# Four gated branches over a Strassen-like input projection on one NeuronCore: merged sums in the loaded buffer, full fp32 memory products, whole-row norms on VectorE, and moved hooks

## What is computed

```python
proj = x @ w_in                       # 1024 -> 10*512 + 4*1024 columns
(q_sb, k_sb, v_sb, g_sb, u_pool, g_pool, u_lru, g_lru, q_xa, g_xa, merge) = _split_columns(proj)
y_sb = stick_breaking_attention(q_sb, k_sb, v_sb) * silu(g_sb)     # 4 heads of 128
y_pool = multiscale_pool(u_pool, w_pool, pool_scale) * silu(g_pool)
y_lru = rg_lru(u_lru, conv_w, conv_b, w_rg, b_rg, w_ig, b_ig, lru_L) * silu(g_lru)
y_xa = memory_cross_attention(q_xa, mem, w_mem_kv) * silu(g_xa)    # k, v = mem @ w_mem_kv
gates = sigmoid(merge.reshape(b, s, 4, 1024))
merged = gates[:, :, 0] * (y_sb @ w_branch[0])
for n in range(1, 4):
    merged = merged + gates[:, :, n] * (branches[n] @ w_branch[n])
out = layer_norm(2 ** 0.5 * x + merged @ w_out, ln_g, ln_b)
```

## Time and profile before

| | |
|---|---|
| median of 2 runs | 2663.57 us (2662.22 to 2664.92) |
| profiled execution, its own time | 2661.26 us |
| its span | 2659.5 us, mean granted PE clock 0.97 |
| PE busy | 2459.5 us, 92% |
| DVE busy | 1598.3 us, 60% |
| ACT busy | 1196.0 us, 45% |
| POOL busy | 1177.7 us, 44% |
| DMA | 257.10 MB, mean 97 GB/s |

### The profile page before, as it was taken

The page is one execution under the profiler, slowest core; times in us unless marked ns, Lnnn a source line. Parts: engine busy times, 40 slices in busy tenths (PEclk is TensorE's granted clock), DMA queues, the critical chain, the costliest instruction groups (busy, mean ns, idle before and its releaser), DMA issues.

```text
span 2659.5 us, 30199 instructions
## 1 busy us (share of the span) xinstructions
PE 2459.5 (92%) x10496; PEld 1955.0 (74%) x10496; DVE 1598.3 (60%) x2060; ACT 1196.0 (45%) x1832; POOL 1177.7 (44%) x764
## 2 busy tenths in 40 slices
PE   6999999999888989999899999999999888989898
PEld 5777778777667767777677777688777667767787
DVE  7677734843774365454787787734843774366354
ACT  5566632332662245222477677733342662245231
POOL 1566544743344333424365555544743344333332
PEclk9999999999999999999999999999999999999999
DMA  5443222123112311262332333222123112312243
GB/s 203 131 130 125 92 95 68 56 103 113 44 61 76 128 41 57 84 261 87 112 108 91 99 115 99 77 83 80 56 103 113 44 62 75 128 45 73 87 158 103
DMA packets 129255, 257.10 MB, mean 97 GB/s; under 512 B 12880, under 2 KB 74320, under 8 KB 128080
## 3 DMA queue, kind: packets, MB, share of 16 engines
q1 hardware_dynamic: 123056, 246.25, 27.5%
q10 hardware_dynamic: 6048, 8.92, 1.0%
HBM read 196.92 MB, written 58.20 MB: 96 GB/s over the span
## 4 chain that ended last, share of the span: by engine, by line
PE 58%; DVE 10%; issue 8%; POOL 4%; DMA 4%; ACT 4%; SPq 0%; ACTq 0%; POOLq 0%; DVEq 0%
PE J L648 11%; PE J L649 11%; PE J L650 11%; PE Z L816 6%; PE ACC L816 3%; PE OB L816 3%; DMA pk_m<-ST 3%; PE OB L786 3%; DVE WL L1529 1%; POOL SR L2034 1%; PE Z L648 1%; PE Z L649 1%; PE Z L650 1%; PE ACC L764 1%; DVE PR L1859 1%
## 5 line engine op out<-in xcount | busy, mean ns | idle before, releaser
L648 PE MATMUL J<-XBH,WHS 128*128 128x512 f32 x1152 | 479.4, 416 | 112.4 <-ACT ST L1031 64.0
L649 PE MATMUL J<-XBL,WHS 128*128 128x512 f32 x1152 | 468.3, 407 | 0.0
L650 PE MATMUL J<-XBH,WLS 128*128 128x512 f32 x1152 | 466.3, 405 | 0.0
L2041 POOL TENSOR_TENSOR WLS<-SR,WHS 128x1024 fp32r<-128x1024 f32 x121 | 319.7, 2642 | 145.0 <-ACT WHS L972 132.5
L648 PEld LDWEIGHTS J<-XBH,WHS 128*128 128x128 f32 x1152 | 228.3, 198 | 180.6 <-ACT ST L1031 72.4
L648 PE MATMUL J<-XBH,WH 128*128 128x512 f32 x864 | 343.4, 398 | 9.5 <-DVE XBL L1469 5.5
L649 PE MATMUL J<-XBL,WH 128*128 128x512 f32 x864 | 337.6, 391 | 0.0
L650 PE MATMUL J<-XBH,WL 128*128 128x512 f32 x864 | 337.0, 390 | 0.0
L1505 DVE TENSOR_TENSOR ST<-J,ST 128x512 f32<-128x512 f32 x160 | 109.5, 687 | 275.5 <-ACT ST L1031 156.8
L650 PEld LDWEIGHTS J<-XBH,WLS 128*128 128x128 f32 x1152 | 228.0, 198 | 50.9
L649 PEld LDWEIGHTS J<-XBL,WHS 128*128 128x128 f32 x1152 | 228.5, 198 | 48.7 <-issue 1.9
(11 more groups left out here) (363 smaller groups left out, 5231.6 us busy)
## 6 DMA issues: line engine op xcount, KB each, us to landing
RAW<-w SPq DMA_DIRECT2D x144, 512.0 KB, 3.7
MB<-pk_m SPq DMA_DIRECT2D x48, 512.0 KB, 6.0
pk_m<-ST SPq DMA_DIRECT2D x42, 512.0 KB, 5.1
KR<-pk_k SPq DMA_DIRECT2D x160, 128.0 KB, 2.2
BRAW<-w SPq DMA_DIRECT2D x64, 256.0 KB, 6.4
VR<-pk_v SPq DMA_DIRECT2D x160, 64.0 KB, 2.0
XRAW<-xt SPq DMA_DIRECT2D x8, 1024.0 KB, 13.1
OR<-w SPq DMA_DIRECT2D x16, 512.0 KB, 6.7
```

Source lines behind the costliest of these rows:

```text
L648: nc.tensor.matmul(to, wh, xh, start=first, stop=True, skip_group_check=True)
L649: nc.tensor.matmul(to, wh, xl, start=False, stop=True, skip_group_check=True)
L650: return nc.tensor.matmul(to, wl, xh, start=False, stop=True, skip_group_check=True)
L2041: G_.tensor_tensor(WLS[:, k, :], SR[:, k, :], WHS[:, k, :].bitcast(F32), ALU.subtract).then_inc(s_lo, 1)
```

## The change

What it does, part by part:

- **Merges.** For n > 0 `add` writes into `MB[f % 2]` in place, and for n = 0 `gated` writes there; stores go out from MB. ACT's first copy into a reused GT waits for the add that read the gate (`merged`, or `mu_done` for n = 0) and no longer for the store. Instead SP's `load_merged` for f >= 2 waits until the store of f-2 from the same MB has landed, and in `exchange` both stores stand ahead of both loads. `gated` of n = 0 waits for the store of f-2.
- **Pool weights** `WPR`, `WPH`, `WPL` and `LNG` get other addresses; WPR is loaded at hook 3 of the first pool pair and split at hook 10.
- **Memory keys and values** are full fp32 matmuls of `MW` and `MRAW` (32 of 256 columns and 16 of 512, in place of 96 and 48), with no splits. CRAW and PRM are loaded last of the first loads. The copy of the values to `VMA` goes from DVE to ACT.
- **Norms.** DVE scales the whole row of 1024; only the last row of all keeps ACT's `scale` and POOL's `finish`. The last two rows of the first half are finished at DVE hooks 2 and 5 of pair 37 (before: one ahead of pair 36, one at its hook 9).
- **First weights of the second half.** POOL makes all four sums, WL, WLS, WL2 and the second WLS between row products, and ACT's splits stand there too; pair 36 then needs none of these from DVE.
- **Hooks.** Mixing (PE) 6 to 8; `memory_turned` 8 to 10 on PE and DVE, `memory_values` 11 to 13, DVE's queries 10 to 11, silu 11 to 12; for n = 2 `split_y` 5 to 3 and `rest_y` 9 to 6.
- **LRU and M2.** The rest of the second weight sum goes from DVE to POOL there; that of the first stays on DVE.

```diff
             def load_merged(half, n, f):
-                wait_kept(sp, half, n - 1, f)
-                wait_if(sp, merged, add_count(half, n, max(f - 1, 0)))
+                if f < 2:
+                    wait_kept(sp, half, n - 1, f + 6)
+                elif n == NB - 1 and f - 2 >= KEPT:
+                    sp.wait_ge(merged, add_count(half, n, f - 1))
+                else:
+                    wait_kept(sp, half, n, f - 2)
                 sp.dma_start(MB[f % 2][:], pk_m[f]).then_inc(mb_in[f % 2], 16)
...
-                sp.dma_start(pk_m[f], GT[f % 4][:]).then_inc(m_kept[f % 4], 16)
+                sp.dma_start(pk_m[f], MB[f % 2][:]).then_inc(m_kept[f % 2], 16)
...
                 for j in (f, f + 1):
                     if n < NB - 1 or j < KEPT:
                         keep_merged(half, n, j)
-                    if n and j + 2 < FT:
-                        load_merged(half, n, j + 2)
+                for j in (f + 2, f + 3):
+                    if n and j < FT:
+                        load_merged(half, n, j)
...
+            def gates_read(half, n, f):
+                if n:
+                    act.wait_ge(merged, add_count(half, n, f) + 1)
+                else:
+                    act.wait_ge(mu_done, f_count(half, n, f) + 1)
...
                 elif kind == "merge" and i >= 2:
-                    wait_kept(act, half, n, 2 * i + p - 4)
+                    gates_read(half, n, 2 * i + p - 4)
...
-                    mm = V_.tensor_tensor(GT[f % 4][:, s], BR[f % 2][c][:], GT[f % 4][:, s], ALU.mult)
+                    to = GT[f % 4][:, s] if n else MB[f % 2][:, s]
+                    mm = V_.tensor_tensor(to, BR[f % 2][c][:], GT[f % 4][:, s], ALU.mult)
...
-                to = MERGED[:, f, :] if n == NB - 1 and f >= KEPT else GT[f % 4][:]
+                to = MERGED[:, f, :] if n == NB - 1 and f >= KEPT else MB[f % 2][:]
...
-                    mm = pass3(KBANK[h][:, 0:MEM], (KWH[h][:, k, :], KWL[h][:, k, :]), (MTH[:, k, :], MTL[:, k, :]),
-                               k == 0)
+                    mm = nc.tensor.matmul(KBANK[h][:, 0:MEM], MW[:, h, k, :], MRAW[:, k, :], start=k == 0,
+                                          stop=k == KD - 1)
...
-                    pair(g0 + POOL0 + h, {6: lambda: mixing(half, h - 1)} if h else {})
+                    pair(g0 + POOL0 + h, {8: lambda: mixing(half, h - 1)} if h else {})
...
-                    pair(g0 + XA0 + h, {8: lambda: memory_turned(half, h - 1),
-                                        11: lambda: memory_values(half, h - 1)} if h else {})
+                    pair(g0 + XA0 + h, {10: lambda: memory_turned(half, h - 1),
+                                        13: lambda: memory_values(half, h - 1)} if h else {})
...
-                    hooks[5] = lambda: split_y(half, n)
+                    hooks[3] = lambda: split_y(half, n)
...
                 if i == 1:
-                    rest_of_second(g)
-                    if quiet(g) or l == 0:
+                    if g != PAIRS:
+                        rest_of_second(g)
+                    if g == 0:
                         rest_of_sums(g, True)
...
-                pair(g0 + 1, {9 if n == 2 else 4: lambda: rest_y(half, n)})
+                pair(g0 + 1, {6 if n == 2 else 4: lambda: rest_y(half, n)})
...
+                n = C if r == HALVES * TB - 1 else D
...
-                V_.scalar_tensor_tensor(RES[t % 3][:, 0:C], RES[t % 3][:, 0:C], ln[:, L_INV:L_INV + 1], LNB[:, 0:C],
+                V_.scalar_tensor_tensor(RES[t % 3][:, 0:n], RES[t % 3][:, 0:n], ln[:, L_INV:L_INV + 1], LNB[:, 0:n],
...
-                if i == 1 and l and not quiet(g):
+                if i == 1 and l:
                     rest_of_sums(g, True)
...
                         pool.wait_ge(wo_dve, 6 * (half + 1))
-                        for j in range(3):
+                        for j in range(4):
                             sum_raw(g0 + PAIRS, j)
                         rest_of_first(g0 + PAIRS)
                         rest_of_sums(g0 + PAIRS, False)
-                        sum_raw(g0 + PAIRS, 3)
-                    if t >= 4:
-                        finish(half, t - 4)
+                        pool.wait_ge(w_hi, 4 * (g0 + PAIRS) + 3)
+                        G_.tensor_tensor(WL2[:], RAW[1][:, 4:8, :], WH2[:].bitcast(F32), ALU.subtract).then_inc(t_lo, 1)
+                        rest_of_sums(g0 + PAIRS, True)
```

More of the change, by code:

```diff
@@ L439, in piece @@
                 head = l < 2 * HEADS
-                if i == 1 and l + 1 < PAIRS and (l or half == 0):
+                if i == 1 and l + 1 < PAIRS and g != PAIRS:
                     load_w(g + 1, 1)
@@ L586, in _, with store_rows @@
             sp.dma_start(vm_keep, VMA[:].rearrange("p h m d -> p (h m d)")).then_inc(mk_kept, 16)
+            def store_rows(half, t):
+                r = half * TB + t
+                sp.wait_ge(o_ready, r + 1)
+                if r == HALVES * TB - 1:
+                    sp.wait_ge(o_rest, 1)
+                sp.dma_start(out[r * P:(r + 1) * P, :], RES[t % 3][:]).then_inc(o_out[t % 3], 16)
             for half in range(HALVES):
@@ L590, in _, with last_rows @@
                 pair(g0)
+                def last_rows():
+                    if half:
+                        for t in (TB - 2, TB - 1):
+                            store_rows(half - 1, t)
                 def first_keys():
@@ L627, in _ @@
                         load_w(g0 + PAIRS, p)
-                for t in range(TB):
-                    r = half * TB + t
-                    if t == TB - 1:
+                for t in range(TB - 2 if half + 1 < HALVES else TB):
+                    if t == TB - 3 and half + 1 < HALVES:
                         for p in range(2):
                             load_w(g0 + PAIRS + 1, p)
-                    sp.wait_ge(o_ready, r + 1)
-                    sp.wait_ge(o_rest, r + 1)
-                    sp.dma_start(out[r * P:(r + 1) * P, :], RES[t % 3][:]).then_inc(o_out[t % 3], 16)
+                    store_rows(half, t)
                     if t + 3 < TB:
@@ L1104, in keys_of @@
                 nc.scalar.copy(KMA[0][:, h, :], KBANK[h][:, 0:MEM]).then_inc(mk_hi, 1)
-            for i in range(2):
-                k = slice(i * KD // 2, (i + 1) * KD // 2)
-                act.wait_ge(m_in[i], 16)
-                nc.scalar.copy(MTH[:, k], MRAW[:, k]).then_inc(m_hi, 1)
-                split_mw(i)
-            split_mw(2)
+            keys_of(0)
+            keys_of(1)
+            first_tile(0)
+            sums_of(0, False)
+            unit_hi(0, 0)
+            unit_hi(0, 1)
+            keys_of(2)
+            keys_of(3)
+            unit_hi(0, 2)
+            unit_hi(0, 3)
             act.wait_ge(c_in, 32)
@@ L2154, in rest_rows, with finish_last @@
                                  ALU.subtract).then_inc(mt_lop, 1)
-            def finish(half, t):
-                pool.wait_ge(scaled, half * TB + t + 1)
-                G_.tensor_tensor(RES[t % 3][:, C:D], RES[t % 3][:, C:D], LNB[:, C:D], ALU.add).then_inc(o_rest, 1)
+            def finish_last():
+                pool.wait_ge(scaled, 1)
+                r = RES[(TB - 1) % 3][:, C:D]
+                G_.tensor_tensor(r, r, LNB[:, C:D], ALU.add).then_inc(o_rest, 1)
             for half in range(HALVES):
                 g0 = half * PAIRS
-                pair(g0, {9: lambda: finish(half - 1, TB - 1)} if half else {})
+                pair(g0)
                 pair(g0 + 1)
@@ L2170, in _ @@
                         pooled(half, h - 1)
-                    pair(g0 + POOL0 + h, {} if h else {5: lambda: pool_weights(half)})
+                    pair(g0 + POOL0 + h, {} if h else {10: lambda: pool_weights(half)})
                 pooled(half, HEADS - 1)
```

255 lines of the change are left out of this document (108 added, 147 removed).

## The result

The changed kernel takes 2591.97 us (median of 2 runs, 2590.30 to 2593.64), against 2663.57 before: a ratio of 0.973, with an interval of 0.969 to 0.977. That is 71.6 us less, where the forecast was 129 less and the range began at 79 less. Timed again, beside the experiments, the same kernel took 2590.96 us against 2657.46, a ratio of 0.976 (0.973 to 0.978); the experiments are compared with this run, which is called c0.

The account below looks back on a forecast made before the run. PE, busy 92% of the span, bounds the kernel with its work, waits and lower clock. 78 + 29 + 5 + 4 + 6 + 10 - 3 = 129 us off 2661.3 gives 2532, as a median 2535 us; range 2505 to 2585.

Parts of the forecast that it names:

- Merges, +78: Merges n = 1 to 3: ACT's wait on the landed store goes, with the low clock behind it; 78 us saved.
- The feared round trip of MB: Merges: store then reload of MB makes adds of tiles 6 and 7 1 to 3 us late; minus 2 in all.
- Memory attention, +29: Transposes two pieces later cover PE's waits for scaled softmax rows: 21.1 us plus 8 of clock, 29 saved.
- LRU, -3: LRU and M2: second weight sum's rest on POOL wins no wait but slows DVE; 3 us lost, between +3 and -22.
- Split of y, +5: M2: earlier split of y halves the 7.8 us wait for YL, with a low stretch; 5 us saved, between 0 and 10.
- Half transition, +10: Pair 36: x splits' waits shrink as DVE has less ahead, ML's wait grows 1.7; 10 us saved, between 5 and 14.
- Start +6: Start: fp32 memory products begin 3.5 us earlier, run 5.5 longer, but splits vanish; 6 us saved, between 0 and 10.
- mixing +4: Mixing on PE two pieces later covers four waits for POOL's PLL, 4.8 us in all; 4 us saved.
- Norms on DVE, 0: Norms: a row costs DVE 0.5 us more for the right 512 columns, PE does not wait for it; 0 us.

Follow-up runs that it names:

- e4: Changed kernel, but ACT's first copy into a reused gate buffer waits again for the landed store: 2658.93 us.
- e7: Changed kernel with M3's four loads of merged sums issued on SP behind the last branch weights: 2579.76 us.
- e8: Changed kernel with the memory attention's hooks as before (transposes at 8) and POOL at rest until the rows PR are scaled: 2586.34 us.
- e3: Changed kernel with POOL in the memory attention waiting ahead of its third weight sum until DVE has scaled the head's rows PR: 2557.51 us.
- e9: Changed kernel plus e3, e6, e7 edits, second sum's rest on DVE in LRU, and POOL waiting in M2's second pair until y is split: 2520.11 us.
- e6: Changed kernel with POOL's rest of the last row tile made ahead of pair 36's weight sums' rests at the half transition: 2583.29 us.

## Why the prediction was wrong

The forecast was 129 us less, the measured gain is 71.6, outside the range. One step failed in its mechanism, the memory attention; most of the others were off in size or rightly sized. Step by step:

- **Merges, +78.** The wait itself: right. 68 measured (e4), 79 with M3's loads out of the way (e7). The prediction looked for late branch weights only behind the last adds, where they "are not due for a pair". It had no term for those of M3's own last branch, right ahead of which SP issues 4 MB. That is the missing 10. The feared round trip of MB cost nothing that shows: DVE's adds into MB stood idle for 3.6 us in all, three times, the longest 1.4, and no wait of PE follows on one.
- **Memory attention, +29.** The failed step, and the largest error, 31 us: the move measured -2.5. The prediction wrote that "DVE's scaling does not depend on those pieces". It does not by semaphores, but POOL's weight sums do, and POOL's start sets how long DVE's scaling takes: 4.24 us and not 1.14. The price of that overlap was put at nothing here. With the collision taken out the step is worth 29 (e8 against e3).
- **LRU, -3.** Measured -8 (6 to 8 by the stages), inside its bounds. The size was off; which of DVE's operations the moved rests stretched was not followed one by one. Two readings in the prediction were off as well: of the 28.7 us of WLS waits 4.2 lie at the start, and PE's long waits in LRU end with the add behind the rest.
- **Split of y, +5.** About 0 by the waits (7.8 us before, 7.4 after; no run has this part alone). In the first half DVE's split began only 0.8 us earlier relative to the moment when PE stood ready, and took 8.98 us for four operations, 8.54 before; POOL worked beside it both times. With POOL held back in e9 the four splits take 4.62 us and no such wait is left.
- **Half transition, +10.** About 5 by the stage table; not run alone. The x splits' waits there fell as forecast (9.6 to 2.1 us, of 16.0 and 5.0 in the whole span). The wait on ML grew by 2.7, which had been put at 1.7, and the whole wait of 7.5 has a price of 8 us with its clock (e6).
- **Start +6, mixing +4.** Start and heads of the first half are 7.6 us shorter in this profile, 4.1 to 6.9 in the twelve other profiles with this start, so about 6. No wait on PLL above 0.3 us is left; the pool stages and M1 of e4, which has the mixing but not the gain of the merges, are 3.3 us shorter than before in all. Neither was tried alone.
- **Norms on DVE, 0.** A row costs DVE 1.4 us more and not 0.5: the whole-row addition of `LNB` takes 1.5 us for 0.75, and the operation with `LNG` 2.4 us for 1.7 at the same size. No wait of PE on it shows.

Sum of these: 68 - 2.5 - 8 + 0 + 5 + 6 + 3 = 71.5, against 71.6 measured. That it comes out so exactly is luck: the last three terms are read from stages, each by a us or two.

In the prediction the slowing of DVE by POOL was weighed for the part that moves work to POOL and nowhere else. But a *hook* moves work in time just as well. The page "SBUF — State Buffer" of the Trainium skill (Who interferes with whom) names tensor_scalar, when its operands meet certain conditions, among the operations that can take the ports shared with GpSimd, the one that comes second being fully blocked. The trace agrees: two of the four scalings end just behind POOL's operations, and the group takes 4.24 us for 1.14. The prediction used the page for two-input operations alone, where it had 0.69 and 2.87 us in its rows.

What stays open: how much of the start's gain is the fp32 products, how the LRU stages could be relieved, and the split of y, the mixing, the start and the half transition as parts of their own.

## What to carry to other kernels

When a hook or wait is moved, list what the *other* engines will start in the time that it frees, and look whether that falls beside the operation that the bound engine waits for and stretches it: here a wait put on GpSimd, which had slack, was worth 33 us. Where DVE itself came late, as in LRU, the same idea gave nothing. After a wait is removed, look at the transfers that the stage needs next: they have come closer by what was won. And two edits that each measure next to nothing may be worth 30 us together, so a factor that looks dead is tried once more with the suspected collision taken out.

## What the runs showed of the hardware

- Four VectorE scalings of 128x256 take 1.14 us alone, 1.9 to 2.2 when GpSimd works beside them for 1.0 to 1.7 us, and 4.0 to 4.3 when it does for 3.4 to 3.9.
- With the memory products in full fp32 PE could start at 6.16 us, held by loads alone (9.60 before), though the keys' products then took 16.3 us against 13.2.
- Of 21 waits of PE of 2.9 to 4.5 us in the kernel before, 20 had a stretch at the lower of the two clock levels begin close to their end; in the changed kernel 9 of 9. A us of such waits was worth 1.3 to 1.5 us: 20.4 us less on PR gave 29 (e8 to e3), 52.7 us less on the ST copy gave 68 (e4 to c0).
